# Up projection in 2x2 block products with seven factors per pair of tiles

## The reference

```python
h2 = _rmsnorm(x, lw['g_ffn']) * (1 + sc2) + sh2
z, conv_new = _causal_dwconv(h2 @ lw['w_up'], conv_prev, lw['w_conv'], lw['b_conv'])
zg, zv = z[..., :D_FF], z[..., D_FF:]
x = x + g2 * ((jax.nn.silu(zg) * zv) @ lw['w_down'])
```

## Time and profile before

| | |
|---|---|
| device time, median of 3 (range) | 2263.23 us (2261.87 to 2264.97) |
| span of the profiled execution | 2262.7 us (its own device time is not listed apart) |
| PE busy | 2216.1 us, 98% |
| DVE, ACT, POOL busy | 1170.1, 874.8, 655.2 us |
| matmuls of the up projection after its first two units, one layer | 2016 |
| granted TensorE clock, mean | 0.995 |

### The profile page before, as it was taken

How to read it: one execution, slowest core, us unless ns; L and a number is a source line. 1 busy time by engine, 2 the same in 40 slices (tenths; PEclk the granted TensorE clock), 3 DMA queues, 4 the chain that set the end, 5 groups by cost and what they waited for, 6 DMA issues and landing times.

```text
span 2262.7 us, 42575 instructions
## 1 busy us (share of the span) xinstructions
PE 2216.1 (98%) x16207; PEld 1987.6 (88%) x16207; DVE 1170.1 (52%) x1831; ACT 874.8 (39%) x1815; POOL 655.2 (29%) x316
## 2 busy tenths in 40 slices
PE   7999999999999999999999999999999999999998
PEld 5899997667789999999988999966677999999998
DVE  4443753844346666651153717457443476666433
ACT  4223225832233555541132332366322355555322
POOL 0223434400022333333322334342000323333332
PEclk9999999999999999999999999999999999999999
DMA  8554332033332222235545433212332422222322
GB/s 301 168 145 99 87 84 65 16 110 108 87 128 91 80 83 83 83 106 165 176 121 179 83 94 82 82 43 61 98 108 58 157 66 84 80 78 83 89 83 84
DMA packets 338278, 230.69 MB, mean 102 GB/s; under 512 B 62732, under 2 KB 321605, under 8 KB 338140
## 3 DMA queue, kind: packets, MB, share of 16 engines
q1 hardware_dynamic: 336594, 226.37, 34.9%
q10 hardware_dynamic: 1546, 2.43, 0.3%
HBM read 223.15 MB, written 5.60 MB: 101 GB/s over the span
## 4 chain that ended last, share of the span: by engine, by line
PE 96%; DVE 2%; ACT 1%; DMA 1%; issue 0%; DVEq 0%; SPq 0%; ACTq 0%
PE PS L1550 62%; PE PS L1518 7%; PE PS L1998 5%; PE PS L2045 5%; PE PS L1910 3%; PE PS L1831 2%; PE PS L1594 2%; PE PS L1646 2%; PE PS L1934 2%; PE PS L1567 1%; PE PS L1887 1%; PE PS L1992 1%; PE PS L1948 1%; PE PS L2074 0%; DMA rows_in<-x_sample 0%
## 5 line engine op out<-in xcount | busy, mean ns | idle before, releaser
L975 POOL TENSOR_TENSOR wlo<-raw,whi 128x1024 fp32r<-128x1024 f32 (+1 forms) x248 | 586.4, 2365 | 1501.8 <-ACT whi L563 1501.8
L563 ACT ACTIVATE whi<-raw 128x1024 fp32r<-128x1024 f32 (+1 forms) x252 | 258.6, 1026 | 926.4 <-PE PS L1550 855.8
L1550 PE MATMUL PS<-h_hi,whi 128*128 128x288 f32 x2496 | 538.2, 297 | 1.3 <-issue 1.1
L1550 PE MATMUL PS<-h_lo,whi 128*128 128x288 f32 x2496 | 534.5, 295 | 0.0
L1550 PE MATMUL PS<-h_hi,wlo 128*128 128x288 f32 x2496 | 534.4, 295 | 0.0
L1550 PEld LDWEIGHTS PS<-h_hi,whi 128*128 128x128 f32 x2496 | 402.2, 188 | 9.8 <-issue 8.9
L1550 PEld LDWEIGHTS PS<-h_lo,whi 128*128 128x128 f32 x2496 | 402.7, 188 | 0.0
L1550 PEld LDWEIGHTS PS<-h_hi,wlo 128*128 128x128 f32 x2496 | 402.5, 188 | 0.0
L1452 DVE TENSOR_SCALAR conv<-zext,convp 128x592 f32<-128x592 f32 x88 | 153.7, 1746 | 135.3 <-ACTq L894 134.9
L1550 PE MATMUL PS<-act_hi,whi 128*128 128x288 f32 x704 | 152.7, 298 | 0.0
L1550 PE MATMUL PS<-act_lo,whi 128*128 128x288 f32 x704 | 150.8, 295 | 0.0
(11 more groups left out here) (286 smaller groups left out, 3314.1 us busy)
## 6 DMA issues: line engine op xcount, KB each, us to landing
raw<-w_up SPq DMA_DIRECT2D x88, 512.0 KB, 3.8
pages<-cache_latent SPq DMA_DIRECT2D x256, 144.0 KB, 2.1
raw<-w_in SPq DMA_DIRECT2D x64, 512.0 KB, 4.0
ada_ring<-w_ada SPq DMA_DIRECT2D x41, 512.0 KB, 4.7
raw<-w_down SPq DMA_DIRECT2D x32, 512.0 KB, 4.0
ada_next<-w_ada SPq DMA_DIRECT2D x17, 512.0 KB, 4.0
ada_first<-w_ada SPq DMA_DIRECT2D x16, 512.0 KB, 10.2
raw<-w_out SPq DMA_DIRECT2D x16, 512.0 KB, 4.7
```

The lines of the kernel that those rows point to most:

```text
L563: nc.scalar.activation(whi[:, slot, 0:width(u)], raw[:, slot, 0:width(u)], ACT.Copy).then_inc(hi_ready.sem, 1)
L975: nc.gpsimd.tensor_tensor(wlo[:, slot, 0:n], raw[:, slot, 0:n], whi[:, slot, 0:n].bitcast(F32), ALU.subtract).then_inc(lo_ready.sem, 1)
L1550: r = mm(PS[0:m, 2 * (j % pairs) + half, 0:HT], w, o[:, k0 + k, half * HT:half * HT + HT], start=(first and k == 0 and part is whi and o i ...
```

## The change

Units 0 to 3 (tile pairs 0 and 1) stay as they were. For each of the 20 pairs p = 2 to 21 the product [gate; value] = W^T h is taken as one of 2x2 blocks: two column tiles of weights (gate, value), two halves of the features (k-tiles 0 to 3 and 4 to 7), two halves of the tokens. It needs seven block products and sums before and after them (Winograd's form of Strassen's method), each of 4 k-tiles x 3 fp32r products = 12 matmuls of 128x288.

- The four sums of activations (T1 to T4) are made once a layer: ACT writes an unrounded copy `hf` of the normalised input, POOL makes the four differences (4x288 columns each), ACT and DVE split them in high and low parts. T1 takes the place of one quarter of `h_hi` and `h_lo`, so it waits for unit 3.
- Per pair, SP loads four quarters of 128x512, DVE makes three sums of weights (`weight_sums`), POOL the fourth (`final_sum`). ACT rounds the 7 x 512 columns in four groups (`pair_hi_group`), POOL subtracts for their low parts (`pair_lo_group`). There are two sets of raw and low parts, and one of high parts, freed group by group.
- PE writes the products to seven banks (one of them in turn 6 or 7), in the order A11, S2, S3, S1, A22, S4, A12. ACT saves the first; DVE adds up the others (`join_*`), with one operand in PSUM each, and puts the results into `zext`.
- The first tap moves from DVE to ACT (`first_tap`), the other two stay on DVE (`other_taps`); their `zext` and `conv` are no longer doubled. The product of gate and value goes to `act_full`. Its split in high and low parts moves to the end of the stage (`act_split` on ACT, `act_rest` on DVE for 15 tiles and on POOL for `POOL_TILES`); the first output tile of the down projection waits for it tile by tile.
- The two conditioning steps of layer 1 move from before the up projection of layer 0 into its down projection.
- Loops of the stage are unrolled; several semaphores elsewhere are merged, and some buffers lie elsewhere.

```diff
+FIRST, LAST = 2, KF - 1
+PAIRS = KF - FIRST
+FACTORS = 7
+A11, S2, S3, S1, A22, S4, A12 = range(FACTORS)
+GROUPS = ((A11, S3), (S3, A22), (A22, A12), (A12, FACTORS))
+P_ORDER = (1, 6, 7, 5, 4, 3, 2)
+POOL_TILES = (2, 3, 5, 7, 9, 11, 15)
...
+                    w = pair_w[p % 2]
+                    sp.wait_ge(sums.sem, sums.at(l, 3 * (p - FIRST)))
+                    quarter(p, a21[0][:], 1, 0, pair_in)
+                    if p == FIRST + 2:
+                        sp.wait_ge(unit_used.sem, unit_used.at(l, U_DOWN))
+                    else:
+                        sp.wait_ge(factor.sem, factor_done(l, p - 2, 1))
+                    quarter(p, w[:, A11], 0, 0, pair_in)
+                    if p > FIRST + 2:
+                        sp.wait_ge(factor.sem, factor_done(l, p - 2, 4))
+                    quarter(p, w[:, A22], 1, 1, pair_in)
+                    if p > FIRST + 2:
+                        sp.wait_ge(factor.sem, factor_done(l, p - 2, 2))
+                    sp.wait_ge(last_sum.sem, last_sum.at(l, p - FIRST))
+                    quarter(p, w[:, A12], 0, 1, a12_in)
+
+                sp.wait_ge(factor.sem, factor_done(l, LAST - 1, 6))
                 for w in range(24):
                     c, m = w % 3, w // 3
...
+                    if k == 1:
+                        nc.scalar.activation(hf[:, f, 0:TP], xn[:, f % 4, 0:TP], ACT.Identity, bias=mod[:, shift + f, 0:1], scale=1.0).then_inc(h_full.sem, 1)
...
+                def first_tap(j, s):
+
+                    f = j + KF * s
+                    cl = conv_last[:, f, :]
                     nc.scalar.drain()
-                    if isinstance(j, int):
-                        hi(l, U_UP + 2 * j + s + 2, 0, s)
-                    else:
-                        hi(l, U_UP + s + 2, j, s)
-                    act.wait_ge(unit_used.sem, unit_used.at(l, 2 * j + (U_UP + s + 1)))
-
...
+                def pair_hi_group(p, g):
+
+                    a, z = GROUPS[g]
+                    if g < 2:
+                        act.wait_ge(sums.sem, sums.at(l, 3 * (p - FIRST) + 2 + g))
+                    else:
+                        act.wait_ge(last_sum.sem, last_sum.at(l, p - FIRST + 1))
+                    if p > FIRST:
+                        act.wait_ge(factor.sem, factor_done(l, p - 1, (6, 5, 3, 2)[g]))
+                    nc.scalar.activation(pair_hi[:, a:z, :], pair_w[pair_set(p)][:, a:z, :], ACT.Copy).then_inc(pair_high.sem, 1)
+
+                def save_first(p):
+
+                    act.wait_ge(factor.sem, factor_done(l, p, 1))
+                    if p >= FIRST + 2:
...
+                for p in range(FIRST + 1, KF):
+                    act.wait_ge(joined.sem, join_done(l, p - 1, C11))
+                    first_tap(p - 1, 0)
+                    pair_hi_group(p, 3)
+                    save_first(p)
+                    if p < LAST:
+                        pair_hi_group(p + 1, 0)
+                    else:
+                        hi(l, U_DOWN, 0, 0)
+                    silu(p - 1)
+                    history(p, 0)
+                    if p < LAST:
+                        pair_hi_group(p + 1, 1)
+                    act.wait_ge(zconv.sem, tile_half(zconv, l, p - 1, 1))
+                    history(p, 1)
+                    if p == LAST:
+                        act.wait_ge(factor.sem, factor_done(l, LAST, 7))
+                        for k in range(6):
+                            act_split(k)
+                    act.wait_ge(joined.sem, join_done(l, p, C21))
+                    first_tap(p, 1)
+                    if p < LAST:
+                        pair_hi_group(p + 1, 2)
...
+                hi(l, U_DOWN + 1, 0, 1)
+                act_split(9)
+                silu(LAST)
+                for k in range(10, KF):
+                    act_split(k)
...
+                def final_sum(p):
+
+                    w = pair_w[pair_set(p)]
+                    pool.wait_ge(a12_in.sem, a12_in.at(l, 16 * (p - FIRST + 1)))
+                    pool.wait_ge(sums.sem, sums.at(l, 3 * (p - FIRST) + 2))
+                    if p >= FIRST + 3:
+                        pool.wait_ge(factor.sem, factor_done(l, p - 2, 3))
+                    nc.gpsimd.tensor_tensor(w[:, S4], w[:, A12], w[:, S2], ALU.subtract).then_inc(last_sum.sem, 1)
+
+                def pair_lo_group(p, g):
+
+                    a, z = GROUPS[g]
+                    w = pair_set(p)
+                    pool.wait_ge(pair_high.sem, group_done(pair_high, l, p, g))
+                    pool.wait_ge(sums.sem, sums.at(l, 3 * (p - FIRST) + 3))
+                    nc.gpsimd.tensor_tensor(pair_lo[w][:, a:z, :], pair_w[w][:, a:z, :], pair_hi[:, a:z, :].bitcast(F32), ALU.subtract).then_inc(pair_low.sem, 1)
...
+                t_difference(b12, b22, b12)
+                nc.gpsimd.drain()
+                t_difference(b22, b22, b11)
+                nc.gpsimd.drain()
                 pool.wait_ge(lo_ready.sem, lo_ready.at(l, U_UP + 3))
                 lo(l, U_UP + 3, 1)
-                with pool.Fori(0, (U_DOWN - U_UP - 4) // 2) as i:
-                    lo(l, U_UP + 4 + 2 * i, 0)
-                    lo(l, U_UP + 5 + 2 * i, 1)
-                for u in range(U_DOWN, UNITS):
+                t_difference(b21, b21, b22)
+                final_sum(FIRST)
+                nc.gpsimd.drain()
+                for g in range(4):
+                    pair_lo_group(FIRST, g)
+                for p in range(FIRST + 1, KF):
+                    final_sum(p)
+                    nc.gpsimd.drain()
+                    for g in range(4):
+                        pair_lo_group(p, g)
+                pool.wait_ge(joined.sem, join_done(l, LAST - 1, C11))
...
+                for k in (2, 3, 5, 7, 9):
+                    act_rest(k)
+                lo(l, U_DOWN + 1, 1)
+                act_rest(11)
+                act_rest(15)
+                lo(l, U_DOWN + 2, 0)
...
+                def weight_sums(p):
+
+                    w = pair_w[pair_set(p)]
+                    first = a21[(p == FIRST) + 0][:]
+                    dve.wait_ge(pair_in.sem, pair_in.at(l, 48 * (p - FIRST + 1)))
+                    if p >= FIRST + 3:
+                        dve.wait_ge(factor.sem, factor_done(l, p - 2, 5))
+                    v.tensor_tensor(w[:, S1], first, w[:, A22], ALU.add).then_inc(sums.sem, 1)
+                    v.drain()
+                    v.tensor_tensor(w[:, S2], w[:, S1], w[:, A11], ALU.subtract).then_inc(sums.sem, 1)
+                    v.tensor_tensor(w[:, S3], w[:, A11], first, ALU.subtract).then_inc(sums.sem, 1)
+
+                def t_low(i, dst, val, high):
+                    dve.wait_ge(t_hi.sem, t_hi.at(l, i))
+                    v.tensor_tensor(dst, val, high.bitcast(F32), ALU.subtract).then_inc(t_lo.sem, 1)
+
+                def other_taps(j, s):
+
+                    f = j + KF * s
+                    c = conv[s][:, 0:ZE - 2]
+                    dve.wait_ge(tap0.sem, tile_half(tap0, l, j, s))
+                    v.scalar_tensor_tensor(c, zext[:, s, 1:ZE - 1], convp[:, 0, f + 2 * KF:f + 2 * KF + 1], c, ALU.mult, ALU.add)
+                    v.drain()
+                    v.scalar_tensor_tensor(c, zext[:, s, 0:ZE - 2], convp[:, 0, f:f + 1], c, ALU.mult, ALU.add).then_inc(zconv.sem, 1)
+
+                def product(j):
+                    v.drain()
+                    dve.wait_ge(silud.sem, silud.at(l, j + 1))
+                    a = act_full[:, j, :]
+                    v.tensor_tensor(a[:, 0:TP], conv[0][:, 0:TP], conv[1][:, 0:TP], ALU.mult)
+                    v.tensor_tensor(by_seq(a[:, TP:T]), by_seq(conv[0][:, ZS:ZE])[:, :, 0:NS], by_seq(conv[1][:, ZS:ZE])[:, :, 0:NS], ALU.mult).then_inc(prod.sem, 1)
+
...
+                def join_u2(p):
+                    dve.wait_ge(saved.sem, saved.at(l, p - FIRST + 1))
+                    dve.wait_ge(factor.sem, factor_done(l, p, 6))
+                    v.tensor_tensor(kept(p, 2), kept(p, 1), PS[:, 1, 0:HT], ALU.add).then_inc(joined.sem, 1)
+
+                def join_u3(p):
+                    v.drain()
+                    dve.wait_ge(factor.sem, factor_done(l, p, 7))
+                    v.tensor_tensor(kept(p, 3), kept(p, 2), PS[:, 2, 0:HT], ALU.add).then_inc(joined.sem, 1)
+
+                def join_c22(p):
+                    v.drain()
+                    dve.wait_ge(factor.sem, factor_done(l, p, 5))
+                    right_half(1, kept(p, 3), PS[:, 6 + p % 2, 0:HT])
+                    v.tensor_tensor(kept(p, 2), kept(p, 2), PS[:, 6 + p % 2, 0:HT], ALU.add).then_inc(joined.sem, 1)
...
+                for p in range(FIRST, KF):
+                    if p > FIRST:
+                        join_c11(p - 1)
+                    if p < LAST:
+                        weight_sums(p + 1)
+                    if p > FIRST:
+                        other_taps(p - 1, 0)
+                    join_u2(p)
+                    product(p - 1)
+                    join_u3(p)
+                    if p == LAST:
```

(40 more changed lines are left out.)

445 lines of the change are left out of this document (287 added, 158 removed).

## The result

The changed kernel takes 2441.72 us (median of 4 runs, 2438.9 to 2443.2) against 2263.14 of the kernel before (4 runs, 2261.87 to 2264.97): 1.078 times as long, 95% interval 1.0755 to 1.0799. The span of the profiled execution is 2439.6 us, 176.9 above before. The forecast was 2418, range 2300 to 2475.

A forecast was written before the change was run, and what follows sets the result against it. PE, busy 98%, bounds the kernel before; afterwards the SBUF port shared by DVE and POOL sets the pairs' pace. 2 x (58 pairs + 7 start + 12 end) + 1 = +155 on 2262.7: 2417.7, median 2418, range 2300 to 2475.

The forecast's parts named there:

- The mechanism: In the pairs, POOL operations and DVE operations with two SBUF inputs exclude each other: 16.10 us against PE's 11.21.
- The pair: Each of 20 up-projection pairs takes 15.7 us instead of 12.81: +58 us a layer.
- the floor: Least exclusive DVE and POOL time a pair if each operation directly followed the other engine's: 13.87 us, +21 a layer.
- 16.2 counted from DVE alone: Pair time from DVE's 11.0 us plus 5.2 of waiting, POOL's 9.77 less 4.6 passing during joins and drains.
- The start: Before the first pair, low weights blocked behind POOL's differences and DVE's weight sums: +7 us a layer, from 0 to 8.
- rival D: PE's clock drops because PE works in short pieces; at half clock a pair takes at least 22.4 us: 2647, 4%.
- The end: First down-projection output tile waits for the activations' late splits and the last pair's work: +12 us a layer, 0 to 20.
- The conditioning steps: They no longer fill PE's gap before the stage and run later: +1.05 us once.
- ACT's extra copy: The copy `hf` fits into ACT's waits in the normalisation: 0, at most 1 us.
- A: Port shared nearly without loss, a pair about 13.9 us, start and end 3 each: 2318, 17%.
- B: PE sets the pairs' pace, both engines working from SBUF at once or lags absorbed by double weight sets: 2202, 10%.
- C: DVE's order makes it worse, joins standing behind taps that wait for ACT; a pair takes 17.5 us: 2498, 6%.

The follow-up runs named there:

- e5: Changed kernel with POOL's pair_lo subtractions replaced by repeated zero fills of about equal length, PE using high parts for low ones: 2238.36 us.
- e3: Changed kernel with DVE's six joins cut to 8 columns each, as many instructions as before, their results left out: 2434.55 us.
- e4: Changed kernel with DVE's second and third taps cut to 8 columns, as many instructions and waits: 2411.22 us.
- e9: Changed kernel with DVE's part of the third unit's low weights put ahead of the first pair's weight sums: 2443.62 us, ratio 1.0789.
- e10: Changed kernel with ten extra matmuls into a spare bank before each of k-tiles 1 to 8 of the first down output tile: 2437.74 us.
- e8: Changed kernel with all 22 low parts of the activations made on DVE and none on POOL: 2440.18 us, ratio 1.0777.
- e11: Changed kernel with all activations' low parts on DVE, tiles 2, 3 and 5 further ahead and four before the last product: 2441.12 us.
- e7: Changed kernel with the fourth weight sum moved from POOL to DVE, behind the gate's taps, same results: 2498.76 us, ratio 1.104.
- e6: Changed kernel with both the joins and DVE's two taps cut to 8 columns, their results left out: 2355.44 us.
- e1: Changed kernel with POOL's pair_lo subtractions replaced by single zero fills of the same columns, PE using high parts for low ones: 2265.57 us.

## Why the prediction was right, and where it was off

**The mechanism** held: DVE and POOL hold each other off SBUF, and the pairs' pace changes from PE to them. In the changed kernel the blocked operations have 1.6 to 2.8 us, the joins 0.45, and e5, which keeps POOL as long at work and takes away its reading, shows that reading is what blocks.

**The pair** was taken at 15.7 us and is 16.15. The working had given three values: the floor 13.87, 14.5 for a port that never pauses, and 16.2 counted from DVE alone, 11.0 + 5.2. The last one fits, but only its second term does so for its reason: the excess of the blocked operations is 5.3 us. The first, 11.0, comes out at 10.85 partly by luck. DVE's own busy time is 277.98 / 20 - 5.3 = 8.6 us a pair and not 10.2, since its joins are shorter than taken and its instructions overlap a little; what fills this up is 19.2 / 16 + 6.0 / 15 = 1.6 us of waits for ACT, for which the working had no term. The step down from 16.2 to 15.7 was a concession to the floor that no row asked for. Over 20 pairs it cost less than it looks, since the second and the last pair take only 12.6 us: the pairs are +63.3 and +63.2 for the +58 forecast, 10.5 of the 24 us that were missed. The end has 8.8 of them, the start 2.1, and 1.6 are the runs' median, which lies 2.1 us above the profiled span and not 0.5. That DVE's round gives the number doesn't make DVE's length the cause: e3 and e4 cut DVE's work by 2.0 and 2.4 us and the pair by 0.2.

**The start** was +7 and is +8, of which some 5.4 us by the mechanism named. In the chain of waits of the changed kernel, ahead of the first pair,

```profile
728.01 3.01 DVE pair_w L1691
731.02 3.04 DVE pair_w L1692
```

stand before the low weights, two sums of 0.69 us each held by a POOL difference of 1152 columns; PE waits 3.7 us for them. The first two units are 1.7 us longer, since PE waits within them for a low part of the activations that takes 2.51 us beside POOL's first difference and 0.75 otherwise. The remaining 2.7 are the half clock of units 2 and 3 behind these waits, which the working had only in rival D. That the sum came near +7 is in so far luck. e9 and e10 show that the +8 can't be had back from there alone.

**The end** was +12 (0 to 20) and is +16.4: 2.5 of gap and 13.9 in the first output tile. The prediction had counted the exclusive work of this place, but not the second row that ends as late, ACT's rounding of the third unit behind its splits and the subtraction after it (e8, e11), nor 2 us of half clock (e10).

**The conditioning steps**, +1.05 by the sum; layer 0's down projection behind its first output tile is 1.5 longer, which may hold them. ACT's extra copy delays the stage by nothing that can be seen: the first up matmul starts at 715.63, before at 715.42. In the pairs' list of waits no DMA stands.

**The rivals.** A (13.9 us a pair) would have needed the engines to hand over without pause; POOL waited 68.5 of 250 us for roundings. B needed both to work from SBUF at once, and is what e5 looks like: its condition decided. Its price was too good, since it left 3 us for both layers' start and end where e5 has 40. C, DVE's order making it worse, had 17.5; e7 comes near it, at 17.74, with both instructions of the product blocked. D: the clock did fall, to 0.95 in the pairs, in short dips, about 115 us of half clock in the whole kernel against 21 before. But the pair's 16.15 us is the same with a dip in it and without, because PE isn't on its path, and what the start loses by the clock the pairs would have lost anyway (e10); only the end paid. The clock and the waits aren't to be counted twice.

## What to carry to other kernels

Before you trade TensorE work for elementwise work, count the pair DVE and POOL in the stage: POOL operations that read SBUF on one side, DVE operations with two SBUF inputs on the other, and lay their orders side by side. Not the sum of their times but who meets whom decides: a DVE instruction of 64 columns that comes a moment late waits for the whole POOL instruction, and taking work off one of two in-order rows moves the meetings elsewhere (e3, e4, e6) or makes them worse (e7). And a stage that keeps its operands a pair longer pays at both ends: here 20 us a layer even without the exclusion in the pairs (e5), more than half of the 32.6 that seven products instead of eight save there.

## What the runs showed of the hardware

A fill on POOL takes 0.955 us for 1024 columns and 0.527 for 512, and doesn't hold a DVE operation with two SBUF inputs: 835 ns, where fills and one reading sum a pair keep POOL busy 184 of 224 us (e5). I had not known from the traces of before that writing alone is free. The Trainium skill (SBUF — State Buffer, "Who interferes with whom") limits its rule on what a DVE operation contends with to POOL instructions that read; e5 agrees, with that number.

The kernel with the longer fills was the faster one: e5 2238.36, e1 2265.57. In e1 POOL, early and waiting for roundings, runs its one reading sum beside a tap each time, as the group of e1 from 850 to 950 us shows:

```profile
L1705 DVE SCALAR_TENSOR_TENSOR conv_g<-zext,convp,conv_g 128x592 f32<-128x592 f32 x9 | 15.4, 1708 | 0.7
```

In e5 that sum falls beside the product, which then takes 0.94 us instead of 0.69. From the first A11 to the down projection it is 236.2 us in e1 and 225.2 in e5 in layer 0: 22 of the 27 us of two layers. So one meeting at another place costs 0.6 us in most pairs and something at their end. That it is the whole cause wasn't tested.
